# A weight stream's ring of eight raw buffers during adaLN, and the RWKV scan's products of a common weight merged to 128 columns

## What is computed

```python
def adaln(cond, ada_w, ada_b):
    m = jax.nn.silu(cond) @ ada_w + ada_b
    return jnp.split(m, 3, axis=-1)

def wkv_scan(s0, r, decay, k, v, kk, b, reverse, emit):
    def step(s, inp):
        r_t, w_t, k_t, v_t, kk_t, b_t = inp
        sa = jnp.einsum('bhij,bhj->bhi', s, kk_t)
        s = s * w_t[:, :, None, :] - sa[..., None] * b_t[:, :, None, :] + v_t[..., None] * k_t[:, :, None, :]
        y = jnp.einsum('bhij,bhj->bhi', s, r_t) if emit else None
        return s, y
```

## Time and profile before

| | |
|---|---|
| runs | 3292.52 us median of 3, 3289.76 to 3297.95 |
| profiled execution | 3299.11 us, of which the span of the trace is 3297.3 |
| matmul records, TensorE | 24050, and as many weight loads |
| busy share | TensorE 89%, VectorE 46%, ScalarE 33%, POOL 2% |
| mean traffic | 74 GB/s over the span |
| stretch of adaLN | 5.7 us (first load) to 115.7 us (last low part) |
| stretch of the scan | 1027.8 us to about 1345 us |

### The profile page before, as it was taken

How to read it: one execution, slowest core, us unless ns; L and a number is a source line. 1 busy time by engine, 2 the same in 40 slices (tenths; PEclk the granted TensorE clock), 3 DMA queues, 4 the chain that set the end, 5 groups by cost and what they waited for, 6 DMA issues and landing times. The chain is left out here.

```text
span 3297.3 us, 55360 instructions
## 1 busy us (share of the span) xinstructions
PE 2921.0 (89%) x24050; PEld 2235.9 (68%) x24050; DVE 1532.5 (46%) x2507; ACT 1074.0 (33%) x1906; POOL 62.1 (2%) x69
## 2 busy tenths in 40 slices
PE   7799988989986887887899999799887998999998
PEld 3478766867855777345788787566655876778876
DVE  5623247353556544655354324455446435354522
ACT  5411367232242333212322223355323323332221
POOL 0000000000000122000000000000000000000000
PEclk9899999989967999788899998899888998999998
DMA  8511200124124111201233222321212112223321
GB/s 271 150 58 51 49 1 2 52 71 134 33 68 133 46 46 36 82 17 51 71 93 95 90 86 68 124 68 43 78 54 64 34 45 98 70 83 91 96 89 64
DMA packets 250179, 243.36 MB, mean 74 GB/s; under 512 B 28248, under 2 KB 218200, under 8 KB 249873
## 3 DMA queue, kind: packets, MB, share of 16 engines
q1 hardware_dynamic: 249634, 238.64, 24.2%
q10 hardware_dynamic: 304, 1.18, 0.1%
HBM read 217.03 MB, written 22.24 MB: 73 GB/s over the span
## 5 line engine op out<-in xcount | busy, mean ns | idle before, releaser
L201 DVE TENSOR_TENSOR second_w_low<-second_w_raw,second_w_high 128x1024 fp32r<-128x1024 f32 (+1 forms) x228 | 272.5, 1197 | 476.8 <-ACT second_w_high L197 476.0
L197 ACT CAST second_w_high<-second_w_raw 128x1024 fp32r<-128x1024 f32 (+1 forms) x228 | 233.0, 1024 | 669.6 <-PE ffn_in_acc L222 253.4
L220 PE MATMUL ffn_in_acc<-ffn_h_high,second_w_high 128*128 128x512 f32 x704 | 281.1, 399 | 14.4 <-DVE ffn_h_low L578 14.4
L222 PE MATMUL ffn_in_acc<-ffn_h_high,second_w_low 128*128 128x512 f32 x704 | 283.0, 402 | 0.0
L221 PE MATMUL ffn_in_acc<-ffn_h_low,second_w_high 128*128 128x512 f32 x704 | 279.7, 397 | 0.0
L201 DVE TENSOR_TENSOR first_w_low<-first_w_raw,first_w_high 128x1024 fp32r<-128x1024 f32 x115 | 140.2, 1223 | 265.5 <-ACT first_w_high L197 265.0
L197 ACT CAST first_w_high<-first_w_raw 128x1024 fp32r<-128x1024 f32 x115 | 120.0, 1047 | 231.8 <-PE attn_in_acc L222 80.2
L220 PEld LDWEIGHTS ffn_in_acc<-ffn_h_high,second_w_high 128*128 128x128 f32 x704 | 133.6, 190 | 49.0 <-issue 17.9
L221 PEld LDWEIGHTS ffn_in_acc<-ffn_h_low,second_w_high 128*128 128x128 f32 x704 | 133.7, 190 | 33.8 <-issue 0.5
L220 PE MATMUL attn_in_acc<-attn_h_high,first_w_high 128*128 128x256 f32 (+1 forms) x416 | 143.7, 345 | 14.3 <-DVE attn_h_low L323 14.3
L222 PEld LDWEIGHTS ffn_in_acc<-ffn_h_high,second_w_low 128*128 128x128 f32 x704 | 133.6, 190 | 31.1
(11 more groups left out here) (808 smaller groups left out, 6363.0 us busy)
## 6 DMA issues: line engine op xcount, KB each, us to landing
second_w_raw<-in_ffn_w_gate SPq DMA_DIRECT2D x44, 512.0 KB, 3.8
second_w_raw<-in_ffn_w_up SPq DMA_DIRECT2D x44, 512.0 KB, 3.8
second_w_raw<-in_ffn_w_down SPq DMA_DIRECT2D x40, 512.0 KB, 3.5
first_w_raw<-in_rec_w_in SPq DMA_DIRECT2D x33, 512.0 KB, 3.9
first_w_raw<-in_attn_ada_w SPq DMA_DIRECT2D x24, 512.0 KB, 4.7
first_w_raw<-in_rec_ada_w SPq DMA_DIRECT2D x24, 512.0 KB, 4.8
second_w_raw<-in_w_in SPq DMA_DIRECT2D x24, 512.0 KB, 3.9
second_w_raw<-in_w_branch_gate SPq DMA_DIRECT2D x24, 512.0 KB, 4.0
```

Of the source, the lines that this page charges most:

```text
L197: act.copy(self.view(self.high[b % self.splits], b), self.view(self.raw[b % self.bufs], b)).then_inc(self.high_done, 1)
L201: dve.tensor_tensor(self.view(self.low[b % self.splits], b), self.view(self.raw[b % self.bufs], b), self.view(self.high[b % self.splits], ...
L220: pe.matmul(out, sh, mh, start=(first and j == 0), stop=False)
L222: ins = pe.matmul(out, sl, mh, start=False, stop=(last and j == len(parts) - 1))
```

## The change

`WeightStream` takes extra raw buffers for one stage. `first_w` gets four more for `adaln`: blocks 0 to 47 use eight buffers, the later ones four, and `start` issues eight loads. The extra buffers are given back after adaLN.

In the scan, `m`, the square and the fourth power lie in one tile `powers`, so that the two products by `a2[:, 1]` (the inverse's step and one half of the fourth power) become one matmul of 128 columns; the other half of the fourth power is made first, into `late`, and gets its 2 I from VectorE at the copy instead of from `constant`. In `inverse` the products by `m` with the off-diagonal part and with the unit matrix become one matmul of 128 columns over a tile `blocks` (off_t beside I). `units` and `twice` are added by VectorE in `four` and `upper`. The copies change hands accordingly: ScalarE and VectorE each take one head of the merged result.

```diff
@@ -132,7 +132,7 @@
-    def __init__(self, nc, stack, name, blocks, bufs=4, splits=3):
+    def __init__(self, nc, stack, name, blocks, bufs=4, splits=3, deep=None):
         def sb(n, dtype):
...
@@ -146,14 +146,20 @@
...
         self.raw = [sb(f"raw{i}", F32) for i in range(bufs)]
+        extra, of = deep if deep is not None else ([], None)
+        self.raw += extra
+        end = self.ranges[of][1] if extra else 0
+        self.ring = [b % len(self.raw) if b < end else b % bufs for b in range(len(self.blocks))]
+        taken = {}
+        self.prior = [(taken.get(i), taken.update({i: b}))[0] for b, i in enumerate(self.ring)]
         self.splits = splits
         self.high, self.low = ([sb(f"{n}{i}", F32R) for i in range(splits)] for n in ("high", "low"))
-        self.landed = [sem(f"w_landed{i}") for i in range(bufs)]
+        self.landed = [sem(f"w_landed{i}") for i in range(len(self.raw))]
         self.high_done, self.split_done = sem("w_high_done"), sem("w_split_done")
-        self.landings, total = [], [0] * bufs
+        self.landings, total = [], [0] * len(self.raw)
         for b, (loads, _, _) in enumerate(self.blocks):
-            total[b % bufs] += 16 * len(loads)
-            self.landings.append(total[b % bufs])
+            total[self.ring[b]] += 16 * len(loads)
+            self.landings.append(total[self.ring[b]])
...
@@ -163,16 +169,16 @@
...
         for b in range(self.loaded, min(upto, len(self.blocks))):
-            if b >= self.bufs:
-                queue.wait_ge(self.split_done, b - self.bufs + 1)
+            if self.prior[b] is not None:
+                queue.wait_ge(self.split_done, self.prior[b] + 1)
             for place, src in self.blocks[b][0]:
-                queue.dma_start(place(self.view(self.raw[b % self.bufs], b)), src
-                                ).then_inc(self.landed[b % self.bufs], 16)
+                queue.dma_start(place(self.view(self.raw[self.ring[b]], b)), src
+                                ).then_inc(self.landed[self.ring[b]], 16)
             self.loaded = b + 1
...
-        self.load(self.nc.sync, self.bufs)
+        self.load(self.nc.sync, len(self.raw))
...
@@ -2220,8 +2226,8 @@
...
                 "value", "solved", "way")
-RWKV_ACT = Marks("four0", "m1", "m2", "m3", "mh", "wx0", "z", "turn0", "turn1", "turn2", "value", "solved", "way")
-RWKV_DVE = Marks("diag_t", "diag", "diag_x", "gram0", "gram1", "square0", "square1", "four1", "eight", "ux0", "ux1", "wx1", "gram_k0", "gram_k1")
+RWKV_ACT = Marks("m1", "m2", "m3", "mh", "wx0", "z", "turn0", "turn1", "turn2", "value", "solved", "way")
+RWKV_DVE = Marks("diag_t", "diag", "diag_x", "gram0", "gram1", "square0", "square1", "four", "m1", "eight", "ux1", "ux0", "wx1", "gram_k0", "gram_k1")
 RWKV_POOL = Marks("first0", "first1", "off")
...
@@ -2242,10 +2248,14 @@
...
         wt = [st.sb(f"way{i}", [P, PAIRS, P]) for i in range(2)]
-        dt, et, dn, m, av, a8, z, mh = (st.sb(n, [P, 2, PAIRS, CH]) for n in (
-            "diag_t", "off_t", "diag", "inv", "value", "eight", "z", "inverse"))
+        dt, dn, av, a8, z, mh = (st.sb(n, [P, 2, PAIRS, CH]) for n in (
+            "diag_t", "diag", "value", "eight", "z", "inverse"))
         near, crossed = st.sb("near", [P, 2, CH]), st.sb("diag_crossed", [P, PAIRS, CH])
-        a2, a4, ux, wx = (st.sb(n, [P, 2, 2, PAIRS, CH]) for n in ("square", "four", "upper", "halved"))
+        ux, wx = (st.sb(n, [P, 2, 2, PAIRS, CH]) for n in ("upper", "halved"))
+        powers = st.sb("powers", [P, 5, 2, PAIRS, CH])
+        m, in_pairs = powers[:, 0], powers[:, 1:5].rearrange("p (a b) h i t -> p a b h i t", b=2)
+        a2, a4 = in_pairs[:, :, 0], in_pairs[:, :, 1]
+        inv_four = powers[:, 0:4].rearrange("p (a b) h i t -> p a b h i t", b=2)[:, :, 0]
         units, twice = st.sb("units", [P, 2, PAIRS, CH]), st.sb("twice", [P, 2, PAIRS, CH])
...
@@ -2278,7 +2288,10 @@
...
-        taken = a4.rearrange("p a h i t -> p (a h i t)")
+        blocks = st.sb("off_t_unit", [P, 2, PAIRS, P])
+        et = blocks[:, :, :, 0:CH]
+        def taken(h):
+            return a4[:, h].rearrange("p h i t -> p (h i t)")
...
@@ -2370,19 +2383,21 @@
...
             def four(n):
-                pe.wait_ge(dve_done, RWKV_DVE(n, "gram1"))
-                constant(early, 256, wide(twice[:, 0]))
                 pe.wait_ge(dve_done, RWKV_DVE(n, "square1"))
-                tiles(early, 0, a2[:, 1], a2[:, 0], 1, 0, start=False)
-                tiles(early, 256, a2[:, 0], a2[:, 1], 1, 0, start=False).then_inc(pe_done, 1)
+                tiles(late, 0, a2[:, 0], a2[:, 1], 1, 0).then_inc(pe_done, 1)
                 pe.wait_ge(pool_done, RWKV_POOL(n, "first1"))
-                tiles(late, 0, a2[:, 1], m, 1, 0).then_inc(pe_done, 1)
+                for i in range(PAIRS):
+                    for h in range(2):
+                        for k in range(2):
+                            r, at = rows(k ^ h), h * BANK + i * P
+                            ins = pe.matmul(early[rows(k), at:at + P], a2[r, 1, h, i, :], powers[r, 0:2, h, i, :],
+                                            start=True, stop=True)
+                ins.then_inc(pe_done, 1)
             def eight(n):
-                pe.wait_ge(act_done, RWKV_ACT(n, "four0"))
-                pe.wait_ge(dve_done, RWKV_DVE(n, "four1"))
+                pe.wait_ge(act_done, RWKV_ACT(n, "m1"))
+                pe.wait_ge(dve_done, RWKV_DVE(n, "m1"))
                 tiles(early, 0, a4[:, 0], a4[:, 1], 0, 1).then_inc(pe_done, 1)
-                pe.wait_ge(act_done, RWKV_ACT(n, "m1"))
                 tiles(late, 0, a4[:, 1], m, 0, 1).then_inc(pe_done, 1)
...
@@ -2391,23 +2406,22 @@
...
             def inverse(n):
+                pe.wait_ge(pool_done, RWKV_POOL(n, "off"))
                 pe.wait_ge(act_done, RWKV_ACT(n, "m3"))
...
                         for k in range(2):
-                            r, to, at = rows(k), rows(k ^ h), h * BANK + i * CH
-                            ins = pe.matmul(late[to, at:at + CH], m[r, h, i, :], eye[r, :], start=True, stop=True)
+                            r, to, at = rows(k), rows(k ^ h), h * BANK + i * P
+                            ins = pe.matmul(early[to, at:at + P], m[r, h, i, :], blocks[r, h, i, :], start=True, stop=True)
                 ins.then_inc(pe_done, 1)
-                pe.wait_ge(pool_done, RWKV_POOL(n, "off"))
-                tiles(early, 0, m, et, 0, 1)
-                tiles(early, 256, et, m, 0, 1).then_inc(pe_done, 1)
+                tiles(late, 0, et, m, 0, 1).then_inc(pe_done, 1)
...
                 pe.wait_ge(act_done, RWKV_ACT(n, "mh"))
-                pe.wait_ge(dve_done, RWKV_DVE(n, "ux1"))
+                pe.wait_ge(dve_done, RWKV_DVE(n, "ux0"))
                 tiles(sa_ps, 0, ux[:, 1], mh, 1, 0, start=False)
...
@@ -2542,7 +2556,7 @@
...
                 pool.wait_ge(dve_done, RWKV_DVE(n, "gram1"))
-                pool.tensor_tensor(all_of(et).rearrange("p (a t) -> p a t", t=CH), all_of(dt).rearrange("p (a t) -> p a t", t=CH),
+                pool.tensor_tensor(et.rearrange("p h i t -> p (h i) t"), all_of(dt).rearrange("p (a t) -> p a t", t=CH),
                                    gb[dr].rearrange("p h i a t -> p (h i) a t")[:, :, 0, :], ALU.subtract).then_inc(pool_done, 1)
...
@@ -2552,12 +2566,12 @@
...
                     a = yt[rows(h)]
-                    ins = pool.tensor_tensor(a, a, block_of(taken, h)[rows(h)], ALU.add)
+                    ins = pool.tensor_tensor(a, a, taken(h).rearrange("p (i t) -> p i t", t=P)[rows(h)], ALU.add)
                 ins.then_inc(own, 1)
...
                     a = yt[rows(h), :, rows(1 - h)]
-                    ins = pool.tensor_tensor(a, a, block_of(taken, 1 - h)[rows(h), :, rows(1 - h)], ALU.add)
+                    ins = pool.tensor_tensor(a, a, taken(1 - h).rearrange("p (i t) -> p i t", t=P)[rows(h), :, rows(1 - h)], ALU.add)
                 ins.then_inc(out_added, 1)
...
@@ -2571,6 +2585,8 @@
...
                 dve.tensor_scalar(twice[:, h], each, 2.0, None, ALU.mult)
+            for h in range(2):
+                dve.tensor_copy(blocks[:, h, :, CH:], each)
             dve.memset(state[:], 0.0).then_inc(cleared, 1)
...
@@ -2604,8 +2620,6 @@
...
                 dve.wait_ge(pe_done, RWKV_PE(n, name))
-                if name == "four" and n > 1 and outs(n - 2):
-                    dve.wait_ge(out_added, outs(n - 2))
                 dve.tensor_copy(to[:, :, 1].rearrange("p a i t -> p a (i t)"),
...
@@ -2618,6 +2632,27 @@
...
                                       units.rearrange("p a i t -> p a (i t)"), ALU.add).then_inc(dve_done, 1)
+
+            def eye_of(m):
+                return eye.rearrange("p (a t) -> p a t", a=1).broadcast_to([P, m, CH])
+
+            def four(n):
+                dve.wait_ge(pe_done, RWKV_PE(n, "four"))
+                if n > 1 and outs(n - 2):
+                    dve.wait_ge(out_added, outs(n - 2))
```

(42 more changed lines are left out.)

## The result

The changed kernel takes 3273.57 us (median of 5 runs, 3261.14 to 3276.37), the kernel before 3297.95 in the 5 runs beside it; the ratio is 0.992, 95% interval 0.990 to 0.994. The profiled execution took 3274.11 us with a span of 3271.5: 25.8 us less span than before, where the steps of the prediction add up to 16.0. So the total hides an error, and a table by stage finds it. Stages end at the start of adaLN's last high part, at TensorE's first record of the scan, at SP's issue of the load that follows the scan, and at the end.

A forecast was written before the change was run, and what follows sets the result against it. Late adaLN was taken as bound by block arrival, the scan mostly by TensorE's instructions in order. Gains of 11.6 + 2 in adaLN and 2.4 in the scan, 16.0 us, taken from 3292.52, gave 3276.5 us; range 3268 to 3287.

The forecast's parts named there:

- Late adaLN: adaLN from 69.12 to 113.39 us: 23 blocks take 1.42 us each instead of 1.925, TensorE the next bound; 11.6 us gained.
- Rival 1: Late adaLN: transfers keep today's 275 GB/s, so adaLN gains 5.5 us; whole time 3284.6 us; chance 15%.
- Start of adaLN: Eight loads ahead of x and ctx: block 8's product at 31.7 us, not 33.80; 2 us gained, between 3 gained and 2 lost.
- the hole moves to block 8: Start of adaLN: TensorE's idle gap before block 4 shifts to before block 8, which arrives at 29.3 us.
- rival 3: Start of adaLN stalls: first high part at 20 us, slow clock at block 8, 1.60 us a block after; 3285.6 us; 8%.
- The scan's columns: TensorE's cost follows columns, so merging saves nothing; dropping the four constant passes a group gains 0.5 us, far end 4.8.
- rival 2: Scan: merging saves a fixed cost per pass, at most 0.44 us a pair, 11 us more; 3266 us; chance 5%.
- The scan's latency: Scan: later copies for `eight` lose 0.8 us in group 0, nothing in groups 1 to 11; DVE's preamble loses 0.5.
- the cover: Scan, groups 1 to 11: the previous group's `scan_new` hides the 0.44 us later copies; without it 4.8 us lost.
- Instruction supply: Scan: 144 of 1,806 instructions a group go, so 8% of 39.6 us of issue waits, 3.2 us gained; ends 0 and 6.4.
- Rivals 3 to 5: The fifth of these: the ring in adaLN does not take effect; excluded by the code, given no chance.
- Rival 4: Scan: shifted packet boundaries raise supply waits to 1.0 us a packet; 31 us slower in all, 3324 us; chance 4%.

The follow-up runs named there:

- front_four: Changed kernel, ring of eight kept, but only four loads issued ahead of x and ctx; last high part of adaLN at 101.14 us, whole time 3256.64 us (single run).
- front_late: Changed kernel with all eight loads issued first and x and ctx behind the barrier; last high part of adaLN at 105.36 us, whole time 3275.05 us (single run).
- unmerged: Changed kernel with each merged product issued as two matmuls of 64 columns, same copies and waits; 3278.94 us, ratio 0.996 to the kernel before.
- the second profile: The changed kernel run once more, unaltered, on another occasion; scan 303.6 us with 23.0 us of issue waits, median 3270.58 us, ratio 0.992.
- shift: Changed kernel plus 32 matmuls of 64 columns in TensorE's idle time of group 0; first run 3254.79 us, repeated median 3260.42 us, ratio 0.990.
- warm_wide: Changed kernel plus 8 matmuls of 256 columns in TensorE's idle time of group 0; median 3260.56 us, ratio 0.990 to the kernel before.
- thin_double: Changed kernel plus 64 matmuls of 8 columns a group from group 1 on, 256 instructions more a group; scan 337.6 us, issue waits 32.4 us.

## Why the prediction was right

**Late adaLN, 11.6 us: right.** 23 x (1.925 - 1.427) = 11.5, and the next bound is TensorE, as said. Rival 1, transfers that keep 275 GB/s, is refuted by 319 GB/s in the same stretch: 0.88 busy was the ring's limit and not the DMA engines'. They are 1.00 busy now, so little is left there.

**Start of adaLN, 2 us: right in size, wrong in mechanism.** Block 8's product came 2.36 us earlier (33.80 to 31.44), from the arrival, as worked out; `front_four` puts the part that comes from issuing all eight first at about 1.4. But the step "the hole moves to block 8" failed, since the one warning that I had put beside it, a stalled issue, came true: first high part at 16.20, inside the 12.4 to 20 that I gave. I took it for a risk only, and rival 3 priced it as 3 us lost where the term's own end is 2. `front_late` shows that the hole with its clock fall, priced by me at up to 2.3 us, would have cost 5.8.

**The scan's columns: right but for 0.1 us a product.** At the upper clock level 64 columns last 15 ns a record against 27 ns for 128, so a merged product of 32 records saves 32 x (2 x 15 - 27) = 0.1 us; the rows at the lower level, on which the prediction went, show 0.02. Over the scan TensorE's own time, with all its waits taken off, is 235.1 us in `unmerged` and 232.7 and 232.9 in the two profiles of the changed kernel: 2.3 us, against the 11 of rival 2, which falls. The 0.5 for the constants cannot be told from the spread. The Trainium skill (TensorEngine Tiling (Array Packing), Instruction Overhead) says that a matmul of one column has the same latency as one of 60. Rival 2 took that for a surcharge on every matmul; it can as well be a floor, and the 8-column matmuls, as slow as those of 64, agree with a floor.

**The scan's latency: wrong by 2.2 us.** The 0.8 and 0.5 lost in group 0 were 3.5 (4.2 in the second profile). The preamble was priced well: the first products of the square start 5.28 us into the scan instead of 4.88, 0.4 later. The added latency was not the cost; TensorE's clock was, since group 0 takes 21.7 us, less than before the change, once the clock is up. The prediction priced group 0 by durations at either level, but took the moment of the rise from the kernel before. The rise came 8 us later. `unmerged` has the same cold group (25.72 us), so merging is not needed for it. What it shares with the changed kernel is that the constants' columns are gone and the waits between products are longer; that this delayed the rise is argued, since no run here put the constants back alone. In groups 1 to 11 the cover held, and no new wait stands before `eight`.

**Instruction supply, 3.2 us: the mis-sized term.** The eleven later groups gained 14.8 us (17.9 by the second profile), of which putting the merged products back takes 11.1 to 14.2. The count was right (144 instructions a group, seven packets in all), the arithmetic behind it was not: I read 39.6 / 84 = 0.47 us as what a packet costs, and took 8% of it. The waits are what is left between a pace of about 3.8 us a packet and TensorE's faster work. Where they are frequent, the group's whole time follows the packets: 8% of a dense group's 26.4 us is 2.1, against 1.5 and 1.8 measured. The upper end of the term, 6.4, came from the same wrong base and did not hold the value. That the forecast of the whole came within 2.9 us is partly luck: against the profiled execution the sum gave 3283.1 where 3274.1 was measured, 9 us off, which is the scan's error. I subtracted from a median of three, 3292.52; the five runs of before have 3297.95, and 16.0 below that would have been 3282, 8.4 us above what was measured.

**Rivals 3 to 5.** The front did stall as rival 3 says, and helped. Rival 4, supply waits that grow by a shift of boundaries, did not occur in any of the changed scans; what a shift does (`shift`, `warm_wide`) is within the spread. Its threshold was summed wrongly: the forecast without the supply term gains 12.8, so the whole gets slower once the mean wait passes 0.47 + 12.8 / 84 = 0.62 us, not 0.70.

## What to carry to other kernels

When "issue" waits come at equal distances, the instruction stream is a pace: count instructions in that stretch and multiply by the pace, not by the mean wait, and take the product as the upper end, since it is saved only where TensorE would otherwise be faster. Here the mean wait gave 3 us, the pace 21, and the runs 11 to 14. Merge products of a common weight there even if columns stay the same, but not into more idle time at the entry of a stage, where TensorE's clock has still to rise. A deeper ring of buffers pays when a stage waits for transfers at a rate that the chip has been seen to exceed; look also at which issue the added loads hold up, because that sets the stage's start.

## What was unexpected of the hardware

- An issue on SP (of ctx) took 4.99 us with eight 512 KB blocks and x queued ahead of it, and 5.02 in `front_late`; with four blocks and x it took 1.81. The next issue there, behind ctx, took 5.10 us in `front_four` and 2.82 in the kernel before. The four long stalls have different lengths but end together, at 15.78, 15.81, 15.59 and 15.59 us.
- A hole of one length cost very different times: after 5.46 us idle (`front_late`) TensorE ran at 1.2 GHz for some 12 us, after 5.62 us in the kernel before for 4.7 us, from 26.11 to 30.76, and after 6.32 us in `front_four` for 3 us, from 26.09. All three had work without a gap behind it. What decides the length is open.
- A matmul of 8 columns holds TensorE as long as one of 64, and in `thin_double` the granted clock fell to 0.92 in groups that ran at 1.00 without them.
- One program's scan moves by 2.4 us (changed kernel) to 8.7 us (`shift`) from run to run, mostly in its issue waits (25.0 and 23.0; 19.4 and 25.1). Over the five profiles with the changed scan it took 297.8 to 306.0.
- Nearly every wait on issue in the scan (486 of 488) ends some 1.4 us after a 16 KB packet of the instruction queue has landed, and such packets start at least 3.2 us apart.
